# A new load order for the expert weights, split gate and up passes, and a last down projection in three column pieces, in a decoder block on one core

## The reference

```python
x = layer_norm(alpha * x + hybrid_mixer(x, ...), ln1_g, ln1_b)
# hierarchical_moe: 4 groups x 8 experts; a token takes the best group and its two best experts
h = silu(einsum('td,edf->tef', xt, w_gate)) * einsum('td,edf->tef', xt, w_up) * combine[..., None]
ffn = einsum('tef,efd->td', h, w_down)          # 32 experts, d = 1024, f = 256
x = layer_norm(alpha * x + ffn, ln2_g, ln2_b)
```

## Time and profile before

| | |
|---|---|
| median of 3 runs | 431.32 us (429.52 to 433.29) |
| profiled execution | 430.34 us |
| its span | 428.4 us |
| granted clock of TensorE, mean share of full | 0.944 |
| TensorE busy (matmul) | 375.0 us, 88% |
| bytes read from HBM | 131.25 MB |

### The profile page before, as it was taken

How to read it: one execution, slowest core, us unless ns; L and a number is a source line. 1 busy time by engine, 2 the same in 40 slices (tenths; PEclk the granted TensorE clock), 3 DMA queues, 4 the chain that set the end, 5 groups by cost and what they waited for, 6 DMA issues and landing times.

```text
span 428.4 us, 7077 instructions
## 1 busy us (share of the span) xinstructions
PE 375.0 (88%) x2829; PEld 276.3 (65%) x2829; DVE 166.1 (39%) x330; ACT 132.0 (31%) x225; POOL 29.5 (7%) x40
## 2 busy tenths in 40 slices
PE   6899899999999999999899993793999796496694
PEld 6899898989899999999655452252355344144143
DVE  2544477777364646446712120055021202012026
ACT  3344454644444444418122121021030212011010
POOL 3000000000000000001000000285200000000004
PEclk9699999999999999999999998697799999599698
DMA  8799885736568686799489999998399999999912
GB/s 285 187 332 356 269 292 168 290 106 206 182 195 295 196 281 200 254 405 422 204 359 424 420 420 422 422 419 353 112 426 420 423 419 423 419 421 419 389 55 98
DMA packets 53998, 132.69 MB, mean 310 GB/s; under 512 B 6610, under 2 KB 39378, under 8 KB 42196
## 3 DMA queue, kind: packets, MB, share of 16 engines
q1 hardware_dynamic: 53908, 132.30, 80.7%
q0 software_dynamic: 64, 0.01, 0.0%
HBM read 131.25 MB, written 1.05 MB: 309 GB/s over the span
## 4 chain that ended last, share of the span: by engine, by line
PE 55%; DMA 25%; DVE 8%; SPq 5%; ACT 3%; issue 2%; POOL 1%; POOLq 0%; ACTq 0%; DVEq 0%
PE bank L1021 24%; DMA dn<-in_w_down 16%; PE bank L1253 7%; PE bank L1281 7%; DMA gu<-in_w_up 6%; PE bank L1139 5%; SPq L362 4%; PE bank L1116 3%; PE bank L1216 3%; DVE wl L722 2%; PE bank L1288 2%; DMA raw<-in_w_in 2%; ACT wh L572 1%; SPq L367 1%; PE bank L1184 1%
## 5 line engine op out<-in xcount | busy, mean ns | idle before, releaser
L722 DVE TENSOR_TENSOR wl<-raw,wh 128x1024 fp32r<-128x1024 f32 x56 | 68.4, 1224 | 70.2 <-ACT wh L572 69.9
L1021 PE MATMUL bank<-xh,wh 128*128 128x256 f32 x288 | 84.1, 292 | 3.5 <-DVE wl L722 3.5
L1021 PE MATMUL bank<-xl,wh 128*128 128x256 f32 x288 | 82.6, 287 | 0.0
L1021 PE MATMUL bank<-xh,wl 128*128 128x256 f32 x288 | 82.5, 286 | 0.0
L572 ACT ACTIVATE wh<-raw 128x1024 fp32r<-128x1024 f32 x56 | 58.7, 1055 | 63.4 <-PE bank L1021 36.6
L1253 PE MATMUL bank<-gu,xg 128*32 128x512 f32 (+1 forms) x576 | 60.5, 576 | 19.7 <-DMA gu<-in_w_up 19.7
L1021 PEld LDWEIGHTS bank<-xh,wh 128*128 128x128 f32 x288 | 56.4, 196 | 6.0 <-DVE wl L722 4.0
L1021 PEld LDWEIGHTS bank<-xl,wh 128*128 128x128 f32 x288 | 56.4, 196 | 0.2 <-issue 0.2
L1021 PEld LDWEIGHTS bank<-xh,wl 128*128 128x128 f32 x288 | 56.4, 196 | 0.0
L1253 PEld LDWEIGHTS bank<-gu,xg 128*32 128x32 f32 x576 | 18.5, 115 | 56.6 <-issue 53.4
L1281 PE MATMUL bank<-dn,hT 128*32 128x512 f32 x232 | 33.5, 678 | 12.7 <-DMA dn<-in_w_down 12.7
(11 more groups left out here) (197 smaller groups left out, 460.9 us busy)
## 6 DMA issues: line engine op xcount, KB each, us to landing
gu<-in_w_gate SPq DMA_DIRECT2D x32, 1024.0 KB, 14.2
gu<-in_w_up SPq DMA_DIRECT2D x32, 1024.0 KB, 23.0
dn<-in_w_down SPq DMA_DIRECT2D x25, 1024.0 KB, 18.5
raw<-in_w_in SPq DMA_DIRECT2D x40, 512.0 KB, 4.7
raw<-in_w_o SPq DMA_DIRECT2D x8, 512.0 KB, 4.6
dn<-in_w_down SPq DMA_DIRECT2D x8, 512.0 KB, 15.9
raw<-in_w_out_conv SPq DMA_DIRECT2D x4, 512.0 KB, 3.6
raw<-in_w_out_attn SPq DMA_DIRECT2D x4, 512.0 KB, 4.5
```

The costliest lines, as they stand in the source:

```text
L722: dve.tensor_tensor(wl[:, s, :].rearrange("p (k c) -> p k c", k=KC), raw[:, pair % NRAW, :].rearrange("p (k c) -> p k c", k=KC) [:, :, n % ...
L1021: mm = pe.matmul(dst, w[:, k, :], v[:, i, :], start=(i == 0 and w is h and v is high_in), stop=(i == len(ks) - 1 and w is l))
```

## The change

1. **Load list.** The gates of quad 2 are loaded in two contraction halves: quad 0's gate products count `gate_ps[0]` after k = 3 and `gate_ps[1]` after k = 7, and each count releases the half that it has read (eight transfers of 512 KB instead of four of 1 MB). Quad 3's loads are parted: gates (after gu of 1), then the fourth dn of 2 and the two norm vectors (after y of 1), then the ups. The down matrices of quad 3 come next (after y of 2), ahead of the gates and ups of quad 4.
2. **Gate and up in two passes** in every quad: the gates go to bank 6, the ups to bank 5, 256 columns each. The sigmoid waits for the gates alone, and so does VectorE's first product.
3. **Last quad.** Its eight transfers have a semaphore each. TensorE makes the gates when they are there, then waits for the ups one by one with four filler matmuls after each of the first three (WARM_LAST), then makes the ups.
4. **Down product in three pieces** (columns 0 to 511, 512 to 767, 768 to 1023; banks 4, 5, 6) in every quad; in the last quad `dn` is loaded in these three pieces (twelve transfers instead of eight), and the order is down 0, down 1, scatter 0, down 2, scatter 1, scatter 2. `ys` of pieces 0 and 2 is copied by ScalarE, of piece 1 by VectorE.
5. **Elsewhere.** `seed(True)` moves from after quad 4 to after quad 6. GpSimd starts on x1n only when `y_ps` is 8 (the second piece of quad 2). The statistics of the first half wait for each tile by itself. GpSimd's shift is one instruction instead of two.

```diff
@@ sync @@
             over = through(1)
-            sp.wait_ge(gate_ps, over)
-            load_gu(0, 2, parts=[0])
+            for i in range(2):
+                ks = slice(i * KHALF, (i + 1) * KHALF)
+                sp.wait_ge(gate_ps[i], over)
+                for e in range(QE):
+                    sp.dma_start(gu0[:, e, 0, ks, :], wg_v[:, 2 * QE + e, ks, :]).then_inc(gate2_in, 16)
...
             sp.wait_ge(gu_ps, through(2))
-            load_gu(1, 3)
-            sp.wait_ge(y_ps, 2 * through(2))
+            load_gu(1, 3, parts=[0])
+            sp.wait_ge(y_ps, NY * through(2))
             for e in range(NE_EARLY, QE):
                 load_dn_one(2, e)
             for i, v in enumerate((ln1_g, ln1_b)):
                 sp.dma_start(ln_row[0:1, i, :], v[0:1, :]).then_inc(ln_in, 16)
+            load_gu(1, 3, parts=[1])
+            sp.wait_ge(y_ps, NY * through(3))
+            load_dn(3)
             for q in range(4, NQ - 1):
                 sp.wait_ge(gu_ps, through(q - 1))
                 load_gu(q % 2, q)
-                if q == 4:
-                    sp.wait_ge(y_ps, 2 * through(3))
-                    load_dn(3)
@@ gpsimd @@
+            pool.wait_ge(rounds_done, 1)
+            pool.wait_ge(y_ps, 2 * pool.value_load(bounds[0:1, 4:5], min_val=1, max_val=MAX_ROUNDS))
@@ tensor, quad @@
+                        for part in range(2):
+                            if last_quad:
+                                pe.wait_ge(bank_free[7], c + 1)
+                                for e in range(QE):
+                                    pe.wait_ge(last_gu_in[part][e], 16)
+                                    if part and e < QE - 1:
+                                        stay_warm(WARM_LAST)
...
+                        down(0)
+                        down(1)
+                        if last_quad:
+                            scatter(0)
+                            down(2)
+                        else:
+                            down(2)
+                            scatter(0)
+                        scatter(1)
+                        scatter(2)
...
-                if q == 4:
+                if q == NQ - 2:
                     pe.wait_ge(x1_done, X1_PARTS)
                     seed(True)
```

More of the change, by code:

```diff
@@ L232, in hybrid_block @@
         ln2_done = sem("ln2_done")
-        dn_cols_in = [sem(f"dn_cols_in{i}") for i in range(2)]
+        dn_cols_in = [sem(f"dn_cols_in{i}") for i in range(NY)]
+        last_gu_in = [[sem(f"last_gu_in{c}{e}") for e in range(QE)] for c in range(2)]
         out_done = sem("out_done")
@@ L290, in hybrid_block @@
         bank_free = {b: sem(f"bank_free{b}") for b in (4, 5, 6, 7)}
+        y_taken = [sem(f"y_taken{i}") for i in range(NY)]
         pick_done = sem("pick_done")
@@ L297, in hybrid_block @@
         put_done = sem("put_done")
-        gate_ps = sem("gate_ps")
+        gate_ps = [sem(f"gate_ps{i}") for i in range(2)]
         gu_ps = sem("gu_ps")
@@ L458, in _ @@
                 load_gu(q % 2, q)
-                if q == 4:
-                    sp.wait_ge(y_ps, 2 * through(3))
-                    load_dn(3)
-                sp.wait_ge(y_ps, 2 * through(q))
+                sp.wait_ge(y_ps, NY * through(q))
                 load_dn(q)
             sp.wait_ge(gu_ps, through(NQ - 2))
[L465 to L468, removed]
+            for c in range(2):
+                load_last_gu(c)
+            sp.wait_ge(y_ps, NY * through(NQ - 1))
+            for i in range(NY):
+                load_dn_cols(i, NQ - 1)
             for t in range(TT):
@@ L984, in _ @@
             compute(last, NQ - 1)
-            dve.wait_ge(added, 4 * total + 2)
+            first = 2 * TT + TT * NY * last
             for t in range(TT):
+                dve.wait_ge(added, first + t + 1)
                 dve.bn_stats(stats[:, t, 0, :], bank[2 * t][:, :])
             for t in range(TT):
-                dve.wait_ge(added, 4 * total + 3 + t)
+                dve.wait_ge(added, first + TT * (NY - 1) + t + 1)
                 link(dve.bn_stats(stats[:, t, 1, :], bank[2 * t + 1][:, :]))
@@ L1235, in dn_of, with quad @@
                 return dn_early[e] if q == 1 and e < NE_EARLY else dn[:, e, :, :]
-            def quad(q, first, half, loads, in_columns):
+            def quad(q, first, half, loads, last_quad):
                     w = gu[half]
@@ L1242, in quad @@
                         pe.wait_ge(bank_free[6], c + 1)
-                        pe.wait_ge(gu_in[half], 2 * QE * 16 * loads)
-                        passes = [slice(0, 1), slice(1, 2)] if q == 0 else [slice(0, 2)]
-                        for part in passes:
+                        if not last_quad:
+                            pe.wait_ge(gu_in[half], 16 * QE * (2 * loads - (half == 0 and loads > 1)))
+                        if q == 2:
+                            pe.wait_ge(gate2_in, 16 * QE * 2)
+                        for part in range(2):
+                            if last_quad:
+                                pe.wait_ge(bank_free[7], c + 1)
+                                for e in range(QE):
+                                    pe.wait_ge(last_gu_in[part][e], 16)
+                                    if part and e < QE - 1:
+                                        stay_warm(WARM_LAST)
                             for k in range(KC):
-                                if part.start == 0 and k < KC // 2:
+                                if part == 0 and k < KC // 2:
                                     pe.wait_ge(xg_a, KC // 2 * c + k + 1)
-                                elif part.start == 0:
+                                elif part == 0:
                                     pe.wait_ge(xg_v, KC // 2 * c + k - KC // 2 + 1)
@@ L1269, in quad, with down @@
                         mm.then_inc(hT_ps, 1)
-                        stay_warm(WARM_ROUND[1], 5)
+                        stay_warm(WARM_ROUND[1], 4)
                         pe.wait_ge(bank_free[7], c + 2)
[L1272 to L1276, removed]
+                        def down(i):
+                            b, lo, hi = Y_PIECES[i]
+                            if last_quad:
+                                pe.wait_ge(dn_cols_in[i], QE * 16)
+                            elif i == 0:
                                 dn_loaded(q)
```

61 lines of the change are left out of this document (37 added, 24 removed).

## The result

The changed kernel takes 419.12 us in the median of four runs (416.84 to 419.82), against 431.10 before (429.52 to 433.29): ratio 0.971, 95% interval 0.9652 to 0.9767. It is faster by 2.9%, 12.0 us. The profiled execution took 419.42 us, its span is 417.3. Against the profiled execution before that is 10.9 us (11.1 of span), where 14.35 were forecast.

A forecast was written before the change was run, and what follows sets the result against it. The second half was taken as one weight-transfer stream at about 420 GB/s with a late start and one hole, then TensorE's tail. Terms 13.9 + 0.15 + 0 + 0.3 = 14.35 off 430.34 gave 416.0 profiled, median 416.5, range 412 to 423.

The forecast's parts named there:

- (a): Quad 2's gates in halves: stream starts 1.75 us earlier, 4 KB rows cost 0.2; gain 1.55, bounds 0.85 to 1.75.
- (b): New load order for quads 3 and 4: the hole in the transfer stream, 298.2 to 307.3 us, goes; gain 9.1 us.
- The rival in which the hole stays: Fourth dn of 2 lands with the ups behind it, stream dry 266 to 275 us: 425.2 us; chance 0.07.
- (c): Quad 3: GpSimd's x1n again runs beside VectorE's work; the same 3.5 us are lost and (b) absorbs them.
- (d): Last quad until the ups start: TensorE, not the transfers, is late; ups start at 391.5, 2.7 us after landing.
- (e): Last quad's gate/up: only the ups remain, 3.55 us where 9.28 were before; gain to this point 13.9 us.
- (f): Last quad: sigmoid and first product moved beside the ups; gain 0.15 us.
- (g): Last quad's down product in three pieces: the third piece's landing just hidden; 0 us, bounds -0.5 to +0.5.
- (h): GpSimd's shift in one instruction, at the kernel's end; gain 0.3 us.
- a fixed cost of about 2.1 us for each transfer: Rival: eight more transfers each hold up the stream, 16.8 us in all: 432.8 us, no change; chance 0.03.
- A clock that stays low: Rival: TensorE's low clock holds in quads 4 to 6 and TensorE becomes the bound: about 464 us; chance 0.03.
- the gain vanishes in other waits: Rival: the stream isn't the bound, the gain of (a) and (b) is lost elsewhere: 424 us; chance 0.04.

The follow-up runs named there:

- e6: The changed kernel with quad 2's gates loaded in four whole transfers after the whole gate pass; one execution, 418.82 us.
- e1: The kernel before with only SyncE's list order changed (quad 3's loads parted, dn of 3 ahead of gu of 4); 420.56 us, ratio 0.9777.
- e3: The changed kernel without the twelve filler matmuls ahead of the last ups (WARM_LAST = 0); 417.02 us, ratio 0.9708.
- e4: The changed kernel with the seed back after quad 4, the fillers kept; 416.24 us, ratio 0.9687.
- e7: The changed kernel with the down product in two column halves in every quad, the last one too; one execution, 417.60 us.
- e5: The changed kernel with GpSimd's shift in two instructions again; one execution, 419.49 us.
- e10: The changed kernel with seed after quad 4, shift in two instructions, and two down pieces (down 0, scatter 0, down 1, scatter 1 in the last quad); 417.21 us, ratio 0.9705.
- e2: The changed kernel with the old order of SyncE's list for quads 3 and 4; 426.54 us, ratio 0.9914.

## Why the prediction was right, and where its sizes were off

The direction, the range and the mechanism were right; 14.35 us were forecast and 11.1 came. The profiled execution was missed by 3.4 us (416.0 against 419.42), the median by only 2.6 (416.5 against 419.12). The difference is luck: the forecast put the median 0.5 us above the profiled execution, and here it lies 0.3 below. By the steps of the forecast:

(a) *Start of the stream*: 1.55 forecast, 0.84 by e6. The bytes began 1.8 us earlier as counted (issue at 212.49 against 214.28), but what the halves cost on the way, taken at 0.2 for their 4 KB rows with bounds 0 to 0.9, was at its upper bound.

(b) *The hole*: 9.1 forecast. From matrix 12 to matrix 57 it was 121.57 us before and 112.32 after: 9.25. y of 2 came at 263.78 (forecast 264.4), matrix 21 only at 267.7 (forecast 266.0), so dn of 3 had some 3 us of cover and not 0.7. A good part of that cover is luck, since it comes from a stream that ran later than counted. The rival in which the hole stays had no ground: the fourth dn of 2 landed at 259.85, ten microseconds ahead of the last of the ups behind it (269.78). e1 isolates this step: 9.3 at matrix 69, 8.2 at the end.

(c) *GpSimd against VectorE*: TensorE waited for hs in quad 3 again, 1.49 us rather than 3.48, and the stream absorbed it, as said.

(d) *Who is late in the last quad*: TensorE, as forecast; e3 and e4 show it from both sides. The ups started at 393.49, forecast 391.5. Of the 2.0 us, 0.5 are bytes (matrix 57 ended at 357.5 and not 357.0), 1.3 are landing: quad 6's products started 3.4 us behind their bytes, and I had counted 2.1 (before the change it was 2.4). How these 1.8 us divide hangs on the count: by the queue of the weights alone the bytes end at 358.1, and the lag is 2.8 where it was 2.1. 1.0 is the clock, 9.80 for gate/up of quad 6 where the row kept was 8.77. Stretches of TensorE in the changed kernel (from:to, length, busy, clock, DMA share, GB/s):

```profile
355.00:360.90 5.90, 0.00 (x0) 0.60 1.01 421
360.90:366.00 5.10, 5.10 (x48) 0.50 1.02 424
366.00:371.00 5.00, 5.00 (x87) 0.96 1.02 419
```

The engine had been idle since 353.4; its clock fell to 0.50 (1.2 GHz) and stayed there for the first 5 us of the products, where before the change it was some 3. The forecast had that as the uncertain term, with 3.5 us as its upper end. That bound was wrong as it was described ("all of it at half clock"): 5.1 us at half clock made the pass 2.7 us longer than at full clock (7.11), so all of it at half clock would cost about 7 us, by this estimate. Smaller things gave 0.8 back (fillers 2.9 and not 3.2, no wait for hs).

(e), (f) 3.60 for the ups as forecast; from their end to the down 2.16 us where 2.4 were counted.

(g) *Three pieces*: 0 forecast within 0.5; measured 9.29 from the down to the last variance, 8.84 before, a loss of 0.45, inside the bound. e7 gives 0.3 of it to the pieces.

(h) *The shift*: +0.3 forecast, -0.6 measured (e5). Here the sign was wrong. I had taken the instruction off the chain and not asked whom GpSimd would meet by being 0.3 us earlier.

Together: 0.5 + 1.3 + 1.0 - 0.8 + 0.05 - 0.25 + 0.45 + 0.9 = 3.15 of the 3.3 us of span between 414.0 and 417.3. The term that failed most is (d), the way from bytes to products in quad 6; its direction was right.

The other rivals: a fixed cost of about 2.1 us for each transfer is refuted by e6, where eight halves in place of four whole transfers cost 0.9 us in all and not 8.4. A clock that stays low did not come: the gate and up products of quads 4, 5 and 6 took 9.62, 9.33 and 9.80 us against 7.11, which is 2.2 to 2.7 us a quad, where the rival needed over 8. That the gain vanishes in other waits is refuted by e1.

## What to carry to other kernels

When a queue works off a list in order, look for the transfer that stands behind more bytes than its consumer can wait for, and put it ahead; here that one swap was worth 8 of 11 us. Then count again who is late: fillers and moved work that were free in a wait stand on the path once the wait is gone (the seed and the fillers, 2 us each; they weren't taken out together, and each alone already runs into the next transfer). A shortened instruction shifts everything behind it, so check which other engine it now runs into.

## What the runs showed that I had not expected

*Landing lags behind the bytes by steps.* The start of a quad's products after a wait, less the end of their last MB: before 2.5, 2.4, 2.3 us for quads 5, 6, 7. In the changed kernel 2.2 for quad 4, then 3.6 and 3.4; in e4 2.1, 3.4, 3.3, 3.0; in e1, with the shorter program, 1.9, 1.8, 1.7 and then 3.0 in quad 7; in e7 and e10 the step comes one quad later than in the changed kernel (2.1 in quad 5, 3.5 in quad 6); in e2, the changed program with the hole, 2.4 and 2.4. (By the queue of the weights alone all are 0.3 to 0.6 less.)

The traces hold a closer look. Each load counts its semaphore sixteen times. I read a count as the end of one of the 16 DMA engines, so the time from the first to the last count of a matrix says how far the engines are apart. Before the change it is 2.0 us up to the hole and 0.40 right behind it (310.56 to 310.96), so the hole does bring the sixteen back into step. But 19 us later it is 1.90 again. In the changed kernel it is 2.4 from quad 2 on, where before the change it was 2.0, and 3.8 at the last of the ups of 5 (loads that share a semaphore hide what is more than a matrix late, except at the last of them). In e1, without a hole, it stays at 1.5 to 1.8 from 225 to 377 us, less than before the change. So a missing hole isn't enough for the step, and a price of 1 us for filling it isn't shown.

Instruction fetches are the likely cause: 16 KB each, about 1.1 us on one engine (25 in the changed kernel, 20 before). Each time that the spread jumps from a small value, a fetch has just run: before the change at 224.10 (0.58 at the landing of 224.06, 1.96 at 227.91) and at 325.72 (0.39 at 325.88, 1.90 at 329.88), in e1 at 221.44 (0.26 at 221.44, 1.55 at 225.22), in e2 at 318.13 (0.47 at 317.71, 1.88 at 321.60). So one fetch leaves one engine some 1.3 to 1.5 us behind, and it stays behind. That the second step, beyond 3 us, is a second fetch on the same engine is only argued; the records do not name the engine, and no run varied the fetches alone.

*The cost of small rows.* The four last down matrices took 10.7 us from matrix 69 to 73 in 2 KB rows before (186.80 to 197.50) and 11.5 in the changed kernel with half of them in 1 KB rows. By the queue of the weights alone it is 11.7 and 12.7.
